# Both output products of a mixing block from three products of rounded parts, and ScalarE scaling the recurrences' outputs by their deviations

## The chip, the cores and the metric

The kernel runs on one core of a Trainium2 chip. The metric is the device time of one execution in microseconds. Times are medians of a few executions of the same program; a profile is one further execution, with its own time. Engine names are those of the profile: PE is TensorE (PEld its weight loads), DVE is VectorE, ACT is ScalarE, POOL is GpSimd, SP is SyncE, which issues most DMA transfers.

## The reference

Two transformer-like blocks on one sequence of 1024 tokens with 1024 features, all in float32. The first block mixes an attention branch and a recurrent branch. What matters here is how their outputs are made and joined:

```python
def direction(dlo, glo, w0_d, w2_d, g2_d, reverse):
    ...
    o = wkv7_scan(rh, heads(decay), kh, vh, -kk, b_vec, reverse)
    o = (head_group_norm(o, ln_g, ln_b) + bonus).reshape(B, S, RWKV_WIDTH)
    g = jax.nn.sigmoid(glo) @ g2_d
    return o.astype(cols.dtype) * g
...
o_b = fwd + bwd
y_a = o_a @ w_o_l[:MLA_WIDTH]          # attention's output, 512 -> 1024
y_b = o_b @ w_o_l[MLA_WIDTH:]          # recurrence's output, 512 -> 1024
gates = jax.nn.sigmoid(gate_cols.reshape(B, S, N_BRANCHES, D) + b_gate[l])
x = x + (gates[:, :, 0] * y_a + gates[:, :, 1] * y_b) @ w_merge[l]
```

`head_group_norm` subtracts each head's mean (8 heads of 64), divides by its deviation, multiplies by a gain and adds a bias. After this come a feed-forward layer, and a second block with gated linear attention, a convolution and another feed-forward layer; the change doesn't touch them.

## The kernel before

The program is written engine by engine: for each engine one function lists its instructions in order, with waits on semaphores (`wait_ge`, L136). Nothing reorders them: an engine that waits holds everything behind it. Tokens go in 8 tiles of 128.

*Recurrences and attention* (about 530 to 1292 us). Two recurrences (forwards `scan(e, 0)`, backwards `scan(e, 1)`) and the attention run at once, as three Python generators per engine which `scans` (L1889) steps in turn: after seven steps that the first recurrence and the attention take ahead, a round is one step of the first recurrence, one of the second, one of the attention. A recurrence has 28 steps for a tile of tokens. So the place of every instruction in an engine's stream is fixed by counting steps. The attention needs fewer steps and ends before the recurrences; its generator then takes one more step, the first part of `outa`. On SyncE that part waits for the attention's end on three engines and for its last stores to `oa_d`, and then loads the attention's output, transposed (`OAT3`, 2 MB), the gate inputs, norm gains, four tiles of `w_o` and four of the gates. On the other engines it does nothing.

*Output stage* (1292 to 1422 us). When both recurrences are over, `var_ve` and `var_ae` make the reciprocal deviations `VR` (one column per direction, tile and head). Then `by_turns` (L1914) alternates two generators on TensorE, VectorE and SyncE:

- `gn_*` handles one token tile, in the order `TORD` = 3, 4, 2, 5, 1, 6, 0, 7. TensorE makes the two directions' gate products and, later, transposes the result. VectorE, for each direction, multiplies by the deviations, by the gain `LG`, adds `bon` (GpSimd's bonus plus bias), multiplies by the gate product in PSUM, and then adds both directions into `acc`. ScalarE copies the transposes out of PSUM, feature-major, into `OBT`.
- `outa_*` is the attention's output product: 16 units (8 feature tiles, 2 halves of the tokens) of four 128x512 float32 products. VectorE multiplies each by its gate from PSUM (an "evacuation") into `mix`.

Four `outa` units go with the first tile, two with each further one. TensorE's transposes of a tile wait for `acc`; they stand in its stream behind the `outa` units of that turn and ahead of the next tile's gate products.

- `outb_*` follows: the recurrence's output product, again 16 units of four float32 products. The last token tile's transposes stand behind its second unit. For each unit VectorE multiplies by the gate (`ty`), adds to `mix`, waits for ScalarE's rounded copy of the sum and subtracts that from the sum (`lo`), so that the merge has its operand in two rounded parts.

SyncE loads `w_o`'s second half during the sixth norm tile, and x again during `outb`. Then comes the merge product (`tok_pe`), whose products are rounded ones (type fp32r) throughout: a value is split into a high part, rounded by a ScalarE copy, and a low part, the difference; the product is the sum of three products, high x high, high x low and low x high. ScalarE and VectorE split the merge's weights, one tile of 128x1024 ahead (`Split`); the tile for TensorE's second step of the merge is split behind VectorE's last `outb` unit.

A float32 product in the source (`mm`, L366) shows as two records in TensorE's timeline, a rounded one as one.

Of the kernel before, what the change touches and what calls it, by code (L numbers as in the profile page):

```python
# [235 lines left out]
def program(nc, a, out):  # L236
    ctx = ExitStack()
    with ctx:
# [11 lines left out]
        room.close()  # L250
        X = region(ctx, "X", 8192)
# [29 lines left out]
        HI.insert(0, region(room, "HI0", 1024, FR))  # L281
        room.close()
# [1527 lines left out]
        GT = [HT[:, 4096 + 512 * i:4608 + 512 * i] for i in range(4)]  # L1810
        WO = [HT[:, 6144 + 512 * i:6656 + 512 * i] for i in range(4)]
        OAT3 = v3(HT[:, 0:4096], 4)
# [4 lines left out]
        OBT = [EX[:, 2048:3072], EX[:, 3072:4096], AR[:, 12288:13312], AR[:, 13312:14336]]  # L1817
        TORD = (3, 4, 2, 5, 1, 6, 0, 7)
        WFIRST = AR[:, 14336:15360]
# [10 lines left out]
        def outa_sp(sp):  # L1830
            def load(n):
                if n >= 4:
                    sp.wait_ge(*at("pe_mix", "a", 2 * (n - 4) + 1))
                sp.e.dma_start(WO[n % 4], a["w_o"][n][:, 0:512]).then_inc(*dma(f"dma_wo{n % 4}", n))

            def gate(i):
                if i >= 4:
                    sp.wait_ge(*at("ve_mix", "a", i - 4))
                sp.e.dma_start(GT[i % 4], g_d[i // 2, i % 2]).then_inc(*dma(f"dma_gt{i % 4}", "a", i))

            for g in ("pe", "ve", "ae"):
                sp.wait_ge(*end("att", g))
# [8 lines left out]
            sp.e.dma_start(G2[1], a["g2"][128:256, :]).then_inc(*dma("dma_ln", "all"))  # L1851
            for n in range(4):
                load(n)
            for i in range(4):
                gate(i)
            yield
            for n in range(8):
# [20 lines left out]
        def outa_ve(ve):  # L1878
            yield
# [23 lines left out]
        def nothing():  # L1903
            while True:
                yield
# [79 lines left out]
        def gn_ae(ae):  # L1985
            stored(ae, 0)
            for t in TORD:
                yield
# [6 lines left out]
            yield  # L1995
# [1807 lines left out]
```

## Time and profile before

| | us |
|---|---|
| median of 3 executions | 3272.03 |
| lowest, highest | 3270.03, 3272.25 |
| the profiled execution | 3276.29 |
| its span, first to last instruction | 3274.5 |

| engine | busy us | share of the span |
|---|---|---|
| TensorE | 3153.8 | 96% |
| VectorE | 2084.6 | 64% |
| ScalarE | 1297.0 | 40% |
| GpSimd | 887.3 | 27% |

Busy time is the sum of an engine's instruction durations; matmul ends are modelled and overlap the next start, so the distance from one start to another is the safer reading of a matmul's price. A row of a timeline gives start, duration, engine, line, operation, output and inputs, and in brackets how long the engine had been idle before it and what released it. Consecutive equal instructions are merged and their number is given (x16).

### The profile page before, as it was taken

What the parts mean: (1) busy time and instruction counts of PE and PEld (TensorE: products, weight loads), DVE (VectorE), ACT (ScalarE), POOL (GpSimd) and SP (SyncE); (2) the same over time, 40 slices, a digit from 0 to 9 for tenths busy, and PEclk for the clock granted to TensorE, in tenths of its full rate; (3) what the DMA queues carried; (4) which work ended last, traced back from release to release, by engine and by line L of the source; (5) the groups of instructions that cost most, each with busy time, mean ns of one, the idle gap of its engine ahead of it and who ended that gap; (6) DMA issues with size and microseconds to landing.
All of it is one profiled execution on the core that took longest, in us unless ns stands there. A gap on an engine that the chain in (4) does not pass through costs nothing.

```text
span 3274.5 us, 61761 instructions
## 1 busy us (share of the span) xinstructions
PE 3153.8 (96%) x26560; PEld 2540.2 (78%) x26560; DVE 2084.6 (64%) x3031; ACT 1297.0 (40%) x2289; POOL 887.3 (27%) x778
## 2 busy tenths in 40 slices
PE   8999999999999988999999999999999999999998
PEld 8678776778887776467888888878677878888887
DVE  5263465666776665847899877762455575565686
ACT  4333334555555432124333344443333343333444
POOL 1232233222322222100576740000000025566100
PEclk9999999999999999999999999999999999999999
DMA  4251245112211121532123247522102322322753
GB/s 151 68 155 49 71 161 178 42 41 64 71 54 46 66 94 44 209 131 91 71 105 117 97 154 247 165 95 89 36 32 74 132 87 85 120 101 97 264 160 116
DMA packets 128016, 346.46 MB, mean 106 GB/s; under 512 B 15792, under 2 KB 19520, under 8 KB 124928
## 3 DMA queue, kind: packets, MB, share of 16 engines
q1 hardware_dynamic: 106592, 258.09, 23.7%
q0 software_dynamic: 21152, 84.42, 6.9%
q8 instruction: 210, 3.44, 0.4%
q14 instruction: 62, 0.51, 0.1%
HBM read 246.51 MB, written 95.94 MB: 105 GB/s over the span
## 4 chain that ended last, share of the span: by engine, by line
PE 83%; DVE 9%; ACT 4%; issue 2%; DMA 1%; POOL 0%; SPq 0%; DVEq 0%; ACTq 0%; POOLq 0%
PE ps L369 42%; PE ps L368 39%; PE ps L372 3%; DVE X L378 2%; DVE AR L378 2%; DVE SM L389 1%; DVE W L378 1%; DVE WS L378 1%; ACT HT L1240 1%; ACT AR L375 1%; DVE EX L378 0%; ACT WS L375 0%; ACT W L2219 0%; DMA AR<-rw_d 0%; DVE HT L382 0%
## 5 line engine op out<-in xcount | busy, mean ns | idle before, releaser
L378 DVE TENSOR_TENSOR WS<-W,WS 128x512 fp32r<-128x512 f32 (+1 forms) x284 | 341.4, 1203 | 251.1 <-ACT WS L375 250.9
L368 PE MATMUL ps<-HH,WS 128*128 128x512 f32 x1280 | 394.1, 389 | 0.0
L368 PE MATMUL ps<-TO,WS 128*128 128x512 f32 x1440 | 345.9, 389 | 0.0
L375 ACT ACTIVATE WS<-W 128x512 fp32r<-128x512 f32 (+1 forms) x284 | 210.0, 740 | 315.2 <-PE ps L369 170.9
L368 PEld LDWEIGHTS ps<-TO,WS 128*128 128x128 f32 x1440 | 270.3, 188 | 56.1
L368 PEld LDWEIGHTS ps<-HH,WS 128*128 128x128 f32 x1280 | 240.2, 188 | 49.9
L368 PE MATMUL ps<-HL,WS 128*128 128x512 f32 x640 | 249.0, 389 | 0.0
L368 PE MATMUL ps<-TO 128*128 128x512 f32 x936 | 226.8, 390 | 0.2 <-DVE TO L378 0.2
L369 PE MATMUL ps<-AR 64*64 64x64 f32 (+2 forms) x5440 | 204.1, 242 | 21.4 <-ACT AR L375 9.6
L368 PE MATMUL ps<-WS 128*128 128x512 f32 x888 | 215.1, 390 | 0.1
L375 ACT ACTIVATE X<-ps 128x512 f32<-128x512 f32 (+1 forms) x168 | 100.5, 598 | 284.5 <-PE ps L369 128.6
L369 PE MATMUL ps<-HL,HI 128*128 128x512 f32 (+1 forms) x512 | 209.1, 408 | 2.8 <-POOL WL L378 2.8
L369 PE MATMUL ps<-WS,HH 128*128 128x512 f32 x640 | 203.0, 393 | 4.5 <-DVE X L378 1.5
L369 PE MATMUL ps<-WS,HL 128*128 128x512 f32 x576 | 206.3, 392 | 0.7 <-DVE X L378 0.7
L369 PE MATMUL ps<-HH,WS 128*128 128x512 f32 (+1 forms) x672 | 205.6, 395 | 1.2 <-ACT HH L375 1.2
L369 PE MATMUL ps<-HH,HI 128*128 128x512 f32 (+1 forms) x512 | 205.7, 402 | 0.0
L369 PE MATMUL ps<-HH,WL 128*128 128x512 f32 (+1 forms) x512 | 205.5, 401 | 0.0
L368 PEld LDWEIGHTS ps<-TO 128*128 128x128 f32 x936 | 175.2, 188 | 37.1 <-DVE TO L378 1.0
L369 PEld LDWEIGHTS ps<-AR 64*64 64x64 f32 (+1 forms) x5440 | 157.1, 137 | 56.7 <-issue 29.2
L368 PEld LDWEIGHTS ps<-WS 128*128 128x128 f32 x888 | 166.3, 188 | 34.8 <-DVE WS L378 0.5
L375 ACT ACTIVATE AR<-ps 128x512 f32<-128x512 f32 (+4 forms) x240 | 124.3, 523 | 164.0 <-PE ps L369 105.2
L378 POOL TENSOR_TENSOR X<-X 128x1024 f32<-128x1024 f32 (+1 forms) x44 | 104.9, 2386 | 296.5 <-DVE X L378 225.4
(367 smaller groups left out, 6409.2 us busy)
## 6 DMA issues: line engine op xcount, KB each, us to landing
AR_b<-h_d SPq DMA_DIRECT2D x154, 256.0 KB, 2.9
AR<-rw_d SPq DMA_DIRECT2D x104, 256.0 KB, 4.1
W<-in_w_fg SPq DMA_DIRECT2D x44, 512.0 KB, 3.8
W<-in_w_fu SPq DMA_DIRECT2D x44, 512.0 KB, 4.9
h_d<-FST POOLq DMA_DIRECT2D x20, 1024.0 KB, 4.4
x_d<-X POOLq DMA_DIRECT2D x24, 512.0 KB, 4.6
W<-in_w_tok SPq DMA_DIRECT2D x24, 512.0 KB, 4.0
rw_d<-X POOLq DMA_DIRECT2D x40, 256.0 KB, 3.3
```

The lines of the kernel that those rows point to most:

```text
L368: return pe.e.matmul(o, l, r, start=start, stop=stop, skip_group_check=True)
L369: return pe.e.matmul(o, l, r, start=start, stop=stop)
L372: return pe.e.transpose(o, i, ident)
L375: return e.e.activation(o, x, ACT.Copy)
L378: return e.e.tensor_tensor(o, x, y, op)
L389: return e.e.tensor_reduce(o, x, AX.X, op)
L1240: ae.e.activation(APB[i % 2], ps[:, b:b + 2, :].rearrange("p a b -> p (a b)"), ACT.Exp, bias=sm(264 + i % 4, 1), scale=SCALE, accum_out=sm ...
```

## The change

Both output products are made from three products of rounded parts in place of one float32 product.

- *Attention's output.* Behind the attention's generator, ScalarE (`att_out_ae`) makes the rounded high part of `OAT3` in eight copies of 128x512, one a step, and GpSimd (`att_out_ge`) the low part in eight subtractions. SyncE's loads of `w_o` and of the gates move from there behind the first recurrence's generator (`wo_first_sp`), where they wait for that recurrence's end on four engines; behind the same generator, after one more step, ScalarE and GpSimd split the first four weight tiles, one a step. The other four are split during the norm tiles (`wo_hi`, `wo_lo`). Weight and gate buffers lie elsewhere.
- *Deviations.* ScalarE multiplies the recurrences' outputs by `VR`, head by head (16 copies of 128x64 with a scale for a tile, two tiles ahead), in place of VectorE's two products per tile.
- *Recurrence's output.* ScalarE copies each transposed tile twice, rounded (`OBH`) and as it is (`OBR`), both now token-tile by token-tile (512 columns in a row), GpSimd subtracts (`OBL`), and TensorE reads the four tiles of a half with a stride (`by_feature`). `w_o`'s second half is split by ScalarE (five copies during the seventh tile, three during the eighth) and GpSimd (`wb_lo`).
- *x again.* The rounded parts lie in x's place, so x is loaded after the last `outb` unit, between the merge's weight loads.

The diff, without the new memory regions and the renamed calls:

```diff
-        GT = [HT[:, 4096 + 512 * i:4608 + 512 * i] for i in range(4)]
-        WO = [HT[:, 6144 + 512 * i:6656 + 512 * i] for i in range(4)]
-        OAT3 = v3(HT[:, 0:4096], 4)
+        GT = [AR[:, 10240 + 512 * i:10752 + 512 * i] for i in range(4)]
+        WO = [AR[:, 8192 + 512 * i:8704 + 512 * i] for i in range(4)]
+        WOL = [WS[:, 512 * i:512 * i + 512] for i in range(4)]
+        WOH = [HL[:, 4096 + 512 * i:4608 + 512 * i] for i in range(4)]
+        OAT3, OAL3, OAH3 = v3(HT[:, 0:4096], 4), v3(HH[:, 0:4096], 4), v3(HH[:, 4096:8192], 4)
-        OBT = [EX[:, 2048:3072], EX[:, 3072:4096], AR[:, 12288:13312], AR[:, 13312:14336]]
+        OBR, OBL = (EX[:, 2048:4096], AR[:, 12288:14336]), (OBL0, OBL1)
+        OBH = (XF[:, 0:2048], XF[:, 2048:4096])
+        WBH = [XF[:, 4096 + 512 * t:4608 + 512 * t] for t in TORD]
+        WBR, WBL = [[z[:, 512 * n:512 * n + 512] for n in range(8)] for z in (W, WL)]
...
+        def by_feature(z):
+            return z.rearrange("p (t k n) -> p k t n", t=4, k=4)
+
...
+        def att_out_sp(sp):
             for g in ("pe", "ve", "ae"):
                 sp.wait_ge(*end("att", g))
...
+        def att_out_ae(ae):
+            for k in range(4):
+                for h in range(2):
+                    ae.wait_ge(*at("dma_oat", 0))
+                    cp(ae, OAH3[:, k, half(h)], OAT3[:, k, half(h)]).then_inc(*ae.sig("ae_mix", "oh", k, h))
+                    yield
+
+        def att_out_ge(ge):
+            for k in range(4):
+                for h in range(2):
+                    ge.wait_ge(*at("ae_mix", "oh", k, h))
+                    tt(ge, OAL3[:, k, half(h)], OAT3[:, k, half(h)], OAH3[:, k, half(h)].bitcast(F32),
+                       ALU.subtract).then_inc(*ge.sig("ge_mix", "ol", k, h))
+                    yield
+
+        def wo_first_sp(sp):
+            for g in ("pe", "ve", "ae", "ge"):
+                sp.wait_ge(*end("scan0", g))
             for n in range(4):
-                load(n)
+                outa_load(sp, n)
             for i in range(4):
-                gate(i)
+                outa_gate(sp, i)
             yield
+
+        def wo_hi(ae, n):
+            ae.wait_ge(*at(f"dma_wo{n % 4}", n))
+            if n >= 4:
+                ae.wait_ge(*at("pe_mix", "a", 2 * (n - 4) + 1))
+            cp(ae, WOH[n % 4], WO[n % 4]).then_inc(*ae.sig("ae_mix", "wh", n))
+
+        def wo_lo(ge, n):
+            ge.wait_ge(*at("ae_mix", "wh", n))
+            tt(ge, WOL[n % 4], WO[n % 4], WOH[n % 4].bitcast(F32), ALU.subtract).then_inc(*ge.sig("ge_mix", "wl", n))
+
+        def wo_first_ae(ae):
+            for n in range(4):
+                yield
+                wo_hi(ae, n)
+
+        def wo_first_ge(ge):
+            for n in range(4):
+                yield
+                wo_lo(ge, n)
+
+        def outa_sp(sp):
             for n in range(8):
                 if n + 4 < 8:
-                    load(n + 4)
+                    outa_load(sp, n + 4)
                 for h in range(2):
                     if 2 * n + h + 4 < 16:
-                        gate(2 * n + h + 4)
+                        outa_gate(sp, 2 * n + h + 4)
                     yield
 
         def outa_pe(pe):
-            yield
             for n in range(8):
-                w3 = v3(WO[n % 4], 4)
+                wh, wl = v3(WOH[n % 4], 4), v3(WOL[n % 4], 4)
                 for h in range(2):
                     b = take(pe, "outa", n, h)
-                    pe.wait_ge(*at(f"dma_wo{n % 4}", n))
-                    pe.wait_ge(*at("dma_oat", 0))
+                    pe.wait_ge(*at("ge_mix", "wl", n))
+                    pe.wait_ge(*at("ge_mix", "ol", 3, 1))
                     for k in range(4):
-                        x = mm(pe, ps[:, b, :], w3[:, k, :], OAT3[:, k, half(h)], k == 0, k == 3)
+                        mm(pe, ps[:, b, :], wh[:, k, :], OAH3[:, k, half(h)], k == 0, False)
+                        mm(pe, ps[:, b, :], wh[:, k, :], OAL3[:, k, half(h)], False, False)
+                        x = mm(pe, ps[:, b, :], wl[:, k, :], OAH3[:, k, half(h)], False, k == 3)
                     x.then_inc(*pe.sig("pe_mix", "a", 2 * n + h))
                     yield
 
...
-        def scans(e, scan, att, outa):
-
-            def att_and_loads():
+        def scans(e, scan, att, after_att, after_first):
+
+            def first_scan():
+                yield from scan(e, 0)
+                e.close("scan0", e.name)
+                yield from after_first(e)
+
+            def att_then():
                 yield from att(e)
                 e.close("att", e.name)
-                next(outa)
-
-            s0, s1, at_ = scan(e, 0), scan(e, 1), att_and_loads()
+                yield from after_att(e)
+
+            s0, s1, at_ = first_scan(), scan(e, 1), att_then()
...
-                    v = VR[:, d * 64 + t * 8:d * 64 + t * 8 + 8]
                     ve.wait_ge(*at(f"dma_of{t}", "all"))
                     ve.wait_ge(*at("dma_ln", "all"))
-                    tt(ve, v3(ot, 8), v3(ot, 8), bl(v, 64), ALU.mult).then_inc(*ve.sig("ve_mix", "n", t, d))
-                    ve.wait_ge(*at("ve_mix", "n", t, d))
+                    ve.wait_ge(*at("ae_mix", "n", t, d))
...
         def gn_ae(ae):
+            def scaled(t):
+                for d in range(2):
+                    ae.wait_ge(*at(f"dma_of{t}", "all"))
+                    ae.wait_ge(*at("ve_mix", "var"))
+                    for h in range(8):
+                        o, v = OF[d][:, t * 512 + 64 * h:t * 512 + 64 * h + 64], d * 64 + t * 8 + h
+                        x = ae.e.activation(o, o, ACT.Copy, scale=VR[:, v:v + 1])
+                    x.then_inc(*ae.sig("ae_mix", "n", t, d))
+
             stored(ae, 0)
-            for t in TORD:
-                yield
+            made = 0
+            scaled(TORD[0])
+            scaled(TORD[1])
+            for n, t in enumerate(TORD):
                 ae.wait_ge(*at("pe_mix", "gT", t))
-                for j in range(2):
-                    x = cp(ae, (EX[:, 2048:4096], AR[:, 12288:14336])[j].rearrange("p (a b) -> p a b", a=2)[:, :, t * P:(t + 1) * P],
-                           v3(ps[:, bank("gnT", t), 256 * j:256 * j + 256], 2))
-                    if j:
-                        x.then_inc(*ae.sig("ae_mix", "gT", t, frees=("gnT", t)))
-            yield
+                cp(ae, of_tile(OBH, t), ps[:, bank("gnT", t), :]).then_inc(*ae.sig("ae_mix", "gh", t))
+                cp(ae, of_tile(OBR, t), ps[:, bank("gnT", t), :]).then_inc(*ae.sig("ae_mix", "gT", t, frees=("gnT", t)))
+                if n < 4:
+                    wo_hi(ae, n + 4)
+                if n + 2 < NT:
+                    scaled(TORD[n + 2])
+                while made < (0, 0, 0, 0, 0, 0, 5, 8)[n]:
+                    ae.wait_ge(*at("dma_wob", 7))
+                    cp(ae, WBH[made], WBR[made]).then_inc(*ae.sig("ae_mix", "bh", made))
+                    made += 1
+
+        def ob_lo(ge, t):
+            ge.wait_ge(*at("ae_mix", "gT", t))
+            tt(ge, of_tile(OBL, t), of_tile(OBR, t), of_tile(OBH, t).bitcast(F32), ALU.subtract).then_inc(*ge.sig("ge_mix", "ob", t))
+
+        def wb_lo(ge, n):
+            ge.wait_ge(*at("ae_mix", "bh", n))
+            tt(ge, WBL[n], WBR[n], WBH[n].bitcast(F32), ALU.subtract).then_inc(*ge.sig("ge_mix", "bl", n))
 
...
+                if n >= 2:
+                    ob_lo(ge, TORD[n - 2])
+                if 1 <= n < 5:
+                    wo_lo(ge, n + 3)
+            wb_lo(ge, 0)
+            ob_lo(ge, TORD[6])
+            for n in range(1, 5):
+                wb_lo(ge, n)
+            ob_lo(ge, TORD[7])
+            for n in range(5, 8):
+                wb_lo(ge, n)
 
...
-                        for t in range(3):
-                            sp.e.dma_start(xt(t), a["x"][t * P:(t + 1) * P, :]).then_inc(*dma(f"dma_x{t}", "again"))
-                    if h == 0 and n >= 3:
-                        sp.e.dma_start(xt(n), a["x"][n * P:(n + 1) * P, :]).then_inc(*dma(f"dma_x{n}", "again"))
+
+        def x_again(sp):
+            sp.wait_ge(*at("pe_mix", "b", 1, 7))
+            for t in range(NT):
+                sp.e.dma_start(xt(t), a["x"][t * P:(t + 1) * P, :]).then_inc(*dma(f"dma_x{t}", "again"))
 
         def outb_pe(pe, gn):
             for h in range(2):
                 for n in range(8):
                     if h == 0 and n == 2:
                         next(gn)
-                    w3 = v3(W[:, 512 * n:512 * n + 512], 4)
+                    wh, wl, oh, ol = v3(WBH[n], 4), v3(WBL[n], 4), by_feature(OBH[h]), by_feature(OBL[h])
                     b = take(pe, "outb", h, n)
-                    pe.wait_ge(*at("dma_wob", 7))
+                    o = v3(ps[:, b, :], 4)
+                    pe.wait_ge(*at("ge_mix", "bl", n))
                     pe.wait_ge(*at("ae_mix", "gT", 7 if h else 0))
                     for k in range(4):
-                        x = mm(pe, ps[:, b, :], w3[:, k, :], OBT[k][:, half(h)], k == 0, k == 3)
+                        mm(pe, o, wh[:, k, :], oh[:, k], k == 0, False)
+                        mm(pe, o, wl[:, k, :], oh[:, k], False, False)
+                    pe.wait_ge(*at("ge_mix", "ob", 7 if h else 0))
+                    for k in range(4):
+                        x = mm(pe, o, wh[:, k, :], ol[:, k], False, k == 3)
                     x.then_inc(*pe.sig("pe_mix", "b", h, n))
...
-            weights_sp(sp, 1, first["1"])
+            weights_sp(sp, 1, 5)
+            x_again(sp)
+            weights_sp(sp, 5, first["1"])
```

## Rows read from the trace of the kernel before

**Rows 1.** The page's part 4: the chain that ended last, share by engine.

```profile
PE 83%; DVE 9%; ACT 4%; issue 2%; DMA 1%; POOL 0%; SPq 0%; DVEq 0%; ACTq 0%; POOLq 0%
```

**Rows 2.** Timeline of TensorE: start, us, engine, line, operation, shapes, count [idle before].

```profile
1310.78 0.66 PE L372 MATMUL ps<-CS,AR 128*128 128x128 f32 x4 [2.70 <-DVE AR L378]
...
1312.99 7.03 PE L369 MATMUL ps<-HT 128*128 128x512 f32 x16
...
1319.86 0.60 PE L372 MATMUL ps<-CS,AR 128*128 128x128 f32 x4
...
1320.30 1.88 PE L369 MATMUL ps<-W,AR 128*128 128x512 f32 x4
...
1322.02 7.03 PE L369 MATMUL ps<-HT 128*128 128x512 f32 x16
...
1364.97 0.60 PE L372 MATMUL ps<-CS,AR 128*128 128x128 f32 x4
...
1422.10 0.79 PE L369 MATMUL ps<-WS,HL 128*128 128x512 f32 x1
```

**Rows 3.** Busy time by stretch: us, then PE, PEld, DVE, ACT, POOL, clock, DMA.

```profile
1700.00:1800.00 100.00, 100.00 (x442) 82.78 (x442) 92.15 (x76) 38.08 (x65) 71.89 (x46) 1.00 0.31 115
```

**Rows 4.** Timeline of VectorE in the norm tiles.

```profile
1322.03 1.64 DVE L378 TENSOR_TENSOR X<-X,W 128x512 f32<-128x512 f32 x1
...
1328.53 1.28 DVE L378 TENSOR_TENSOR AR<-HT,ps 128x512 f32<-128x512 f32 x2
...
1332.11 0.69 DVE L378 TENSOR_TENSOR X<-X,AR 128x512 f32<-128x512 f32 x1
```

**Rows 5.** Timeline of GpSimd in the norm tiles.

```profile
1321.53 1.59 POOL L378 TENSOR_TENSOR AR<-AR,W 128x512 f32<-128x512 f32 x1
...
1328.76 1.04 POOL L378 TENSOR_TENSOR AR<-AR,SM 128x512 f32<-128x512 f32 x1 [5.64 <-DVE AR L378]
...
1347.26 1.27 POOL L378 TENSOR_TENSOR AR<-AR,W 128x512 f32<-128x512 f32 x1
```

**Rows 6.** Timeline of ScalarE, and of SyncE's queue at 1137.34, in the recurrences.

```profile
1135.65 0.60 ACT L375 ACTIVATE X<-ps 128x512 f32<-128x512 f32 x1 [0.49 <-PE ps L369]
...
1137.34 0.37 SPq L1845 DMA_DIRECT2D HT<-oa_d  x1
...
1138.25 0.63 ACT L1714 ACTIVATE AR<-AR 128x512 f32<-128x512 f32 x1 [2.00 <-DVE AR L378]
...
1144.07 0.60 ACT L375 ACTIVATE AR<-ps 128x512 f32<-128x512 f32 x1 [1.16 <-PE ps L369]
...
1281.07 0.38 ACT L375 ACTIVATE AR<-ps 128x256 f32<-128x256 f32 x1 [3.69 <-PE ps L369]
```

**Rows 7.** DMA issues, 1136 to 1142: count, KB each, us from issue to landing.

```profile
HT<-oa_d SPq DMA_DIRECT2D x1, 2048.0 KB, 8.0
```

**Rows 8.** Timeline of TensorE and GpSimd behind the attention's end.

```profile
1140.48 0.59 PE L369 MATMUL ps<-AR 64*64 64x64 f32 x13 [1.51 <-ACT AR L375]
...
1143.14 2.54 POOL L378 TENSOR_TENSOR AR<-AR 128x512 f32<-128x512 f32 x2 [7.91 <-PE ps L368]
...
1146.05 1.09 PE L372 MATMUL ps<-CS,AR 128*128 128x128 f32 x8
...
1154.82 0.33 PE L368 MATMUL ps<-AR,X 128*64 128x64 f32 x3 [1.67 <-issue]
```

**Rows 9.** Groups of instructions, shapes apart: count | busy us, mean ns | idle before.

```profile
L375 ACT ACTIVATE HL<-AR 128x512 fp32r<-128x512 f32 x12 | 7.6, 630 | 27.4 <-DVE AR L378 27.4
...
L375 ACT ACTIVATE W<-ps 64x128 f32<-64x128 f32 x32 | 8.7, 272 | 13.0 <-PE ps L369 12.6
...
L378 POOL TENSOR_TENSOR SPLIT<-AR,SPLIT 128x512 fp32r<-128x512 f32 x14 | 18.8, 1343 | 36.5 <-ACT SPLIT L375 36.5
```

**Rows 10.** Busy time by stretch, as Rows 3.

```profile
1156.00:1160.00 4.00, 4.00 (x84) 2.70 (x78) 1.94 (x5) 1.44 (x3) 0.00 (x0) 0.66 1.05 390
```

**Rows 11.** Timeline of VectorE at the end of the first recurrence.

```profile
1279.00 0.69 DVE L389 TENSOR_REDUCE SM<-AR 128x8 f32<-128x512 f32 x1 [1.15 <-POOL AR L378]
```

**Rows 12.** Line 1834 (loads of w_o, 256 KB): its eight landings.

```profile
DMA to landing us min/median/max: 3.2/7.9/11.4
```

**Rows 13.** Timeline of VectorE in the recurrence's output units.

```profile
1376.45 0.68 DVE L378 TENSOR_TENSOR W<-HT,ps 128x512 f32<-128x512 f32 x1
...
1379.16 0.68 DVE L378 TENSOR_TENSOR W<-HT,ps 128x512 f32<-128x512 f32 x1
...
1425.77 1.23 DVE L378 TENSOR_TENSOR WS<-W,WS 128x1024 fp32r<-128x1024 f32 x1 [0.26 <-ACT WS L375]
```

More of the change, by code:

```diff
@@ L250, in program @@
         room.close()
+        room = ExitStack()
+        XF = region(room, "XF", 8192, FR)
+        room.close()
         X = region(ctx, "X", 8192)
@@ L281, in program @@
         HI.insert(0, region(room, "HI0", 1024, FR))
+        room.close()
+        room = ExitStack()
+        region(room, "AR_e", 4096)
+        OBL1 = region(room, "OBL1", 2048, FR)
+        region(room, "AR_f", 8192 + 2048)
+        OBL0 = region(room, "OBL0", 2048, FR)
         room.close()
@@ L1828, in half, with of_tile, outa_load, outa_gate @@
             return slice(512 * h, 512 * h + 512)
[L1830 to L1839, printed above, removed]
+        def of_tile(z, t):
+            return z[t // 4][:, 512 * (t % 4):512 * (t % 4) + 512]
+        def by_feature(z):
+            return z.rearrange("p (t k n) -> p k t n", t=4, k=4)
+        def outa_load(sp, n):
+            if n >= 4:
+                sp.wait_ge(*at("pe_mix", "a", 2 * (n - 4) + 1))
+            sp.e.dma_start(WO[n % 4], a["w_o"][n][:, 0:512]).then_inc(*dma(f"dma_wo{n % 4}", n))
+        def outa_gate(sp, i):
+            if i >= 4:
+                sp.wait_ge(*at("ve_mix", "a", i - 4))
+            sp.e.dma_start(GT[i % 4], g_d[i // 2, i % 2]).then_inc(*dma(f"dma_gt{i % 4}", "a", i))
+        def att_out_sp(sp):
             for g in ("pe", "ve", "ae"):
@@ L1852, in outa_sp @@
+        def wo_first_sp(sp):
+            for g in ("pe", "ve", "ae", "ge"):
+                sp.wait_ge(*end("scan0", g))
             for n in range(4):
-                load(n)
+                outa_load(sp, n)
             for i in range(4):
-                gate(i)
+                outa_gate(sp, i)
             yield
+        def wo_hi(ae, n):
+            ae.wait_ge(*at(f"dma_wo{n % 4}", n))
+            if n >= 4:
+                ae.wait_ge(*at("pe_mix", "a", 2 * (n - 4) + 1))
+            cp(ae, WOH[n % 4], WO[n % 4]).then_inc(*ae.sig("ae_mix", "wh", n))
@@ L1857, in outa_sp @@
+        def wo_lo(ge, n):
[7 more added lines that the diff above has]
+            for n in range(4):
+                yield
+                wo_lo(ge, n)
+        def outa_sp(sp):
             for n in range(8):
                 if n + 4 < 8:
-                    load(n + 4)
+                    outa_load(sp, n + 4)
@@ L1901, in scans, with nothing @@
             e.close("scans", e.name)
-        def nothing():
-            while True:
-                yield
+        def nothing(e):
+            return iter(())
         def scans_done(e):
@@ L1985, in gn_ae @@
         def gn_ae(ae):
+            def scaled(t):
[6 more added lines that the diff above has]
+                    x.then_inc(*ae.sig("ae_mix", "n", t, d))
             stored(ae, 0)
-            for t in TORD:
-                yield
+            made = 0
+            scaled(TORD[0])
+            scaled(TORD[1])
+            for n, t in enumerate(TORD):
                 ae.wait_ge(*at("pe_mix", "gT", t))
-                for j in range(2):
-                    x = cp(ae, (EX[:, 2048:4096], AR[:, 12288:14336])[j].rearrange("p (a b) -> p a b", a=2)[:, :, t * P:(t + 1) * P],
-                           v3(ps[:, bank("gnT", t), 256 * j:256 * j + 256], 2))
-                    if j:
-                        x.then_inc(*ae.sig("ae_mix", "gT", t, frees=("gnT", t)))
-            yield
+                cp(ae, of_tile(OBH, t), ps[:, bank("gnT", t), :]).then_inc(*ae.sig("ae_mix", "gh", t))
[14 more added lines that the diff above has]
+            tt(ge, WBL[n], WBR[n], WBH[n].bitcast(F32), ALU.subtract).then_inc(*ge.sig("ge_mix", "bl", n))
         def gn_ge(ge):
@@ L3581, in tensor_program @@
             prep_pe(pe)
-            scans(pe, scan_pe, att_pe, outa)
+            scans(pe, scan_pe, att_pe, nothing, nothing)
             gn = gn_pe(pe)
@@ L3610, in vector_program @@
             prep_over(ve)
-            scans(ve, scan_ve, att_ve, outa)
+            scans(ve, scan_ve, att_ve, nothing, nothing)
             scans_done(ve)
@@ L3638, in scalar_program @@
             prep_over(ae)
-            scans(ae, scan_ae, att_ae, nothing())
+            scans(ae, scan_ae, att_ae, att_out_ae, wo_first_ae)
             scans_done(ae)
             var_ae(ae)
-            for _ in gn_ae(ae):
-                pass
+            gn_ae(ae)
             outb_ae(ae, sp)
@@ L3667, in gpsimd_program @@
             prep_over(ge)
-            scans(ge, scan_ge, att_ge, nothing())
+            scans(ge, scan_ge, att_ge, att_out_ge, wo_first_ge)
             scans_done(ge)
@@ L3687, in sync_program @@
             prep_sp(sp)
-            scans(sp, scan_sp, att_sp, outa)
+            scans(sp, scan_sp, att_sp, att_out_sp, wo_first_sp)
             gn = gn_sp(sp)
```

## The prediction

> **What bounds the kernel now.** I read the page's chain first: TensorE holds 83% of what ended last [rows 1]. The changed code lies between 1133 and 1430 us, so each price below is read there, stage by stage.
>
> *The output stage* (1292 to 1422). In TensorE's timeline [rows 2] the attention's output products are f32, two records each: 16 records, eight products, start at 1312.99 and the next instruction at 1319.86, so 0.859 us a product. A tile of the group norm takes 9.02 us (the first transposes at 1310.78, the seventh set at 1364.97: 54.19 for six), all of it TensorE: 0.44 transposes, 1.72 gate products (1319.86, 1320.30, 1322.02), 6.86 output products. The recurrence's products follow, 16 units of 3.43 us, to 1422.10, 57.1 after the seventh transposes. What a rounded product costs is read where nothing else runs: 442 in 100 us [rows 3], at most 0.227 us each.
>
> VectorE is nearly as full there. A norm tile has nine operations of 0.69 (1332.11 [rows 4]), a pitch of 0.72, and two evacuations: 8.0 us. It stretches to about 9 because GpSimd gets in the way, and the rows give the pattern: GpSimd's operation of 1321.53 [rows 5] lasts 1.59 instead of 1.27 (1347.26) and ends at 1323.12; VectorE's, started at 1322.03, lasts 1.64 and ends at 1323.67, that is, it runs its 0.55 after GpSimd's end. They take turns, about 1.1 us for GpSimd and 0.55 for VectorE. VectorE's operations with an input from PSUM are spared: two at 1328.53 take 1.28 beside GpSimd's of 1328.76. The Trainium skill, "SBUF — State Buffer", section "Who interferes with whom", says the same: a VectorE instruction with two inputs in SBUF and a GpSimd instruction that reads SBUF shut each other out for a whole instruction. It speaks against this change, which adds GpSimd operations of just this kind; the trace agrees with it, and the sums below use the rows' 1.1 and 0.55.
>
> *The recurrences* (to 1292). There the chain hops between TensorE, ScalarE and VectorE, and a delay of an in-order engine goes straight into the end.
>
> **The change part by part.**
>
> 1. *Products.* 64 + 64 f32 products become 384 rounded ones: 128 x (0.859 - 3 x 0.227) = -22.8 us of TensorE. A norm tile falls to 0.44 + 1.72 + 24 x 0.227 = 7.6, an output unit from 3.43 to 2.73. That is an upper bound; parts 4 and 5 say what is left of it.
>
> 2. *The attention's rounding, in the recurrences' stream.* ScalarE now makes eight rounded copies directly after the attention's last step, one per round of the interleaved generators. After the attention's last copy its order [rows 6] is one step of each recurrence (ending with 1135.65), then the exponentials at 1138.25. The first new copy stands between these two, and it waits for the whole reload of the attention's output. That load was issued at 1137.34, after the stores that it reads, and landed 8.0 us later [rows 7]: 1145.35. With the copy's 0.63 the exponentials start at 1146.0, 7.75 late. TensorE can't fill this: it already waits 1.51 us for the copy behind the exponentials (1140.48 [rows 8]). So +7.75.
>
>    Behind it, GpSimd's eight subtractions, 1.27 (as those of 1143.14) to 1.34 [rows 8, 9] each, queue ahead of its recurrence work. The fourth waits for ScalarE's fourth copy, which stands behind that of 1144.07 (then 1151.8), so it runs to about 1154.2; the two products of 1143.14, shifted to 1150.9, start only then and end at 1156.6. TensorE wants the first for the transposes of 1146.05 (then 1153.8), the second half-way: +2.3. The squares and the next sums, behind further subtractions, give +0.6 and +0.9. Bounds 0 (if all of it finds gaps) and 5.
>
>    Clock: after TensorE's 1.67 us without work before 1154.82, put down to issue [rows 8], the mean granted clock was 0.66 in 1156 to 1160 [rows 10], between the levels of 2.4 and 1.2 GHz: 0.34 x 4 = 1.4 us of work lost. A 9 us wait should bring one such stretch, +1.4. The old wait and its stretch, -1.7 - 1.4, should go, since eight loads that filled the queues at that time move to part 3. Bounds of the three together: -3.5 to +3.
>
>    Sum 7.75 + 3.8 - 1.7 = **+9.9** (4.3 to 15).
>
> 3. *First weights, at the end of the recurrences.* SyncE's four weight and four gate loads wait for the first recurrence on every engine; the last is VectorE's reduction of 1279.00, ended 1279.69 [rows 11]. This load landed in 3.2 at its fastest [rows 12]; in the quiet here I take 2.8, so 1282.6. ScalarE's first weight copy (0.63 [rows 9]) stands right ahead of the second recurrence's copy of 1281.07 [rows 6]: that goes to 1283.2, **+2.2** (1.5 to 3). The other three copies fit into ScalarE's waits that follow.
>
> 4. *Norm tiles.* VectorE loses two operations of nine. ScalarE gains 16 scalings of 128x64 a tile; no row has one, the nearest is 0.272 for 64x128 [rows 9], so at most 4.4 a tile; with two copies from PSUM and a weight copy it stays under 6.3 and runs two tiles ahead: hidden. (The Trainium skill, "ScalarE: Activation LUTs", section "What ACT_TABLE_LOAD costs", has a formula by which these would follow each other every 0.24 us, 3.8 a tile: the same verdict.) First tile: TensorE's first four units end 2.9 earlier, but the tile waits for its load and now for eight scalings, about 2 us, in which VectorE waited for GpSimd anyway: I get the first sum 0.9 earlier, **-0.9** (-2 to 0).
>
>    From there GpSimd has four operations a tile (three from the sixth on) in place of two. Worked through in turns: the second tile, with four evacuations first, costs VectorE 2.5, seven operations and three lost turns, 10.3 instead of 9.08; the next three 7.85 each; the last two 8.1. Sum 50.05 against 54.19: **-4.1**. Bounds: TensorE's own 7.6 throughout, -8.5, and -1.
>
> 5. *The recurrence's products.* The first unit waits for a copy and a subtraction of its weights after the seventh transposes, 1.8 us; the second 0.6; the last transposes come 9.9 after the seventh. TensorE would finish 48.6 after the seventh transposes instead of 57.1. But VectorE's units [rows 13] are 2.71 us long without GpSimd (1376.45 to 1379.16), as long as TensorE's 2.73, and begin late: the first needs a ScalarE copy that stands behind the last weight copies (13.2 after the seventh transposes), and the next three take turns with GpSimd's seven subtractions. VectorE starts unit five at 23.2 and, never catching up, ends at 57.2. The merge's second weight split comes behind it (now 1.23 at 1425.77, just in time) and is done at 59.0; TensorE wants it at 54.1. So the merge resumes 3.6 us earlier than now: **-3.6** (-8.5 to -1).
>
> 6. *x reloaded later.* SyncE issues eight loads of 512 KB after the last unit, ahead of the merge's fifth later weight load. At the rate of the reload of 2048 KB [rows 7] they take 16 us at most; the merge's first evacuation needs x only after 96 products, 21.8 us, its fifth later split at 27: nothing.
>
> **Sum.** 9.9 + 2.2 - 0.9 - 4.1 - 3.6 = +3.5. The profiled execution took 3276.29 (span 3274.5), 4.3 above the median of 3272.03; I add to the median: 3275.5.
>
> **Rivals.**
> A. *GpSimd hides.* If the subtractions mostly meet VectorE's PSUM operations and waits, TensorE bounds the stage: -8.5 in part 4, -8.5 in part 5, total 9.9 + 2.2 - 0.9 - 17 = -5.8, 3266. For it: two evacuations and two of seven operations are spared. Against: the turns [rows 4, 5].
> B. *Slower, from the recurrences.* GpSimd's late products make both recurrences wait again, and the old issue wait stays: part 2 at 15, part 3 at 3, the rest as forecast: +9.4, 3281; with VectorE's late start also 3 worse, 3284. It decides once part 2 exceeds 13. For it: eight subtractions of 1.3 us in as many rounds, each ahead of recurrence work. Against: GpSimd has long waits there (7.91 before 1143.14 [rows 8]).
> C. *The products aren't at the rounded price.* The recurrence's moving operand is now read as four pieces of 128 columns; at half the rate 192 products cost +44, 3316. Against: the pieces are long.
>
> **How the numbers follow.** Forecast 0.57, A 0.2, B 0.2, C 0.03. A measurement of this kernel tells 0.2%, 6.5 us, from no change. Beyond -6.5 lies half of A and a sliver: 0.12. Beyond +6.5 lie B, C and the upper tail of the forecast (0.09): 0.32. Within: 0.56. Range: from A's time to B's upper one, 3266 to 3284.
>
> **What would show it.** Right: a ScalarE wait of about 8 us on the attention's reload near 1137, with TensorE idle; TensorE's last recurrence product some 12 us later than now; norm tiles of about 8 us, ended by VectorE; VectorE operations of 1.2 us and more beside GpSimd; a TensorE wait of some 5 us on the merge's second split. Wrong: norm tiles of 7.6 with TensorE unbroken (A); a delay at the end of the recurrences far from 12 us (parts 2, 3); rounded products slower than 0.227 in the recurrence's units (C).

## The result and the profile after

The changed kernel takes 3277.31 us (median of 18 runs, 3272.40 to 3281.47), the kernel before on the same chips 3271.84 (18 runs). The ratio is 1.0018, 95% interval 1.0011 to 1.0025: 5.5 us slower. The interval lies clear of 1, but the difference is less than the 0.2% named ahead as what can be told from no change. The profiled execution took 3274.67, span 3272.7. A single span is no measure of so small a change: the attention's last copy by ScalarE comes at 1125.32 in it and at 1133.55 before, and in all ten profiles of this case it lies between these two, though the change touches no instruction ahead of it. So both traces are read from that copy on, stage by stage.

The page of the changed kernel, part 1 (busy us, share, instructions) and the first line of part 4 (as [rows 1]):

```profile
PE 3133.3 (96%) x26688; PEld 2565.4 (78%) x26688; DVE 2086.3 (64%) x3015; ACT 1343.0 (41%) x2441; POOL 935.4 (29%) x810
...
PE 82%; DVE 9%; ACT 4%; issue 2%; DMA 2%; POOL 0%; SPq 0%; DVEq 0%; ACTq 0%
```

TensorE did lose work, and the time didn't follow. The timeline of ScalarE around the attention's end and at the recurrences' end (the counterpart of [rows 6]):

```profile
1125.32 0.28 ACT L384 ACTIVATE HT<-ps 128x128 f32<-128x128 f32 x1 [2.17 <-PE ps L378]
...
1139.05 0.63 ACT L384 ACTIVATE HH<-HT 128x512 fp32r<-128x512 f32 x1 [11.03 <-DMA HT<-oa_d]
1139.58 0.61 ACT L1723 ACTIVATE AR<-AR 128x512 f32<-128x512 f32 x1
...
1288.12 0.63 ACT L384 ACTIVATE HL<-AR 128x512 fp32r<-128x512 f32 x1 [5.09 <-DMA AR<-in_w_o]
```

The first rounded copy keeps ScalarE waiting 11.03 us for the reload, and the exponentials of L1723 stand behind it: 14.26 us after the attention's last copy instead of 4.70. Line 1867, the reload (the counterpart of [rows 7]):

```profile
DMA to landing us min/median/max: 9.9/9.9/9.9
```

The timeline of GpSimd, and of TensorE and VectorE (the counterparts of [rows 8, 11]); the last two lines are the first recurrence's last reduction and the gates' first product:

```profile
1148.32 1.27 POOL L387 TENSOR_TENSOR HH<-HT,HH 128x512 fp32r<-128x512 f32 x1 [3.56 <-ACT HH L384]
1149.55 2.93 POOL L387 TENSOR_TENSOR AR<-AR 128x512 f32<-128x512 f32 x2
...
1141.80 0.97 PE L378 MATMUL ps<-AR 64*64 64x64 f32 x13 [11.06 <-ACT AR L384]
...
1150.86 0.66 PE L381 MATMUL ps<-CS,AR 128*128 128x128 f32 x4 [1.69 <-POOL AR L387]
...
1284.66 0.69 DVE L398 TENSOR_REDUCE SM<-AR 128x8 f32<-128x512 f32 x1 [1.15 <-POOL AR L387]
...
1299.91 1.98 PE L378 MATMUL ps<-W,AR 128*128 128x512 f32 x4 [0.40 <-DVE W L387]
```

The two products that TensorE needs stand behind a subtraction until 1149.55. Busy time by stretch (columns as [rows 3]; the clock is the third number from the right):

```profile
1135.00:1140.00 5.00, 0.00 (x0) 0.00 (x0) 0.00 (x0) 0.95 (x2) 0.23 (x1) 0.55 1.02 396
1140.00:1145.00 5.00, 3.20 (x64) 3.12 (x66) 2.37 (x3) 2.96 (x7) 3.53 (x3) 0.50 0.39 145
1145.00:1150.00 5.00, 4.18 (x94) 3.74 (x90) 2.82 (x6) 3.03 (x6) 1.69 (x2) 0.93 0.01 2
1150.00:1155.00 5.00, 3.03 (x46) 2.49 (x50) 2.82 (x4) 0.79 (x2) 5.00 (x5) 0.76 0.15 56
1155.00:1160.00 5.00, 4.82 (x134) 4.36 (x126) 4.22 (x10) 2.77 (x8) 5.00 (x6) 0.90 0.81 249
```

While TensorE stands still the granted clock falls to its level of 1.2 GHz (0.50), and the first 3.9 us of work behind the wait, to 1145.7, run at it. Behind the waits of 1.69 us (1150.86) and 1.11 us (1152.62) it falls to that level a second time, for 3.4 us until 1156.

The timeline of TensorE in the output stage (the counterpart of [rows 2]): first, second, third and seventh transposes, and the merge's second weight:

```profile
1317.75 1.11 PE L381 MATMUL ps<-CS,AR 128*128 128x128 f32 x4 [4.93 <-DVE AR L387]
...
1328.12 0.60 PE L381 MATMUL ps<-CS,AR 128*128 128x128 f32 x4
...
1335.77 0.60 PE L381 MATMUL ps<-CS,AR 128*128 128x128 f32 x4
...
1366.47 0.66 PE L381 MATMUL ps<-CS,AR 128*128 128x128 f32 x4
...
1425.77 0.79 PE L378 MATMUL ps<-WS,HL 128*128 128x512 f32 x1 [4.26 <-DVE WS L387]
```

From the second tile on there is no wait ahead of the transposes: 7.65 us a tile. VectorE and GpSimd beside it (the counterparts of [rows 4, 5]), then VectorE's first output unit and the merge's splits (the counterpart of [rows 13]):

```profile
1330.98 1.31 DVE L387 TENSOR_TENSOR X<-X,W 128x512 f32<-128x512 f32 x1
1332.32 1.42 DVE L387 TENSOR_TENSOR X<-X,AR 128x512 f32<-128x512 f32 x1
...
1330.44 1.29 POOL L387 TENSOR_TENSOR WS<-AR,HL 128x512 fp32r<-128x512 f32 x1 [3.74 <-ACT HL L384]
1331.70 1.49 POOL L387 TENSOR_TENSOR AR<-AR,SM 128x512 f32<-128x512 f32 x1
...
1330.25 3.93 ACT L2058 ACTIVATE X<-X,SM 128x64 f32<-128x64 f32 x16
...
1380.28 1.06 DVE L387 TENSOR_TENSOR ML<-AR,HL 128x512 fp32r<-128x512 f32 x1 [4.51 <-ACT HL L384]
...
1424.49 2.36 DVE L387 TENSOR_TENSOR WS<-W,WS 128x1024 fp32r<-128x1024 f32 x2 [0.25 <-ACT WS L384]
```

The stretches by these marks, in us. The kernel before is read at the rows shown ahead of the prediction and at these rows of ScalarE and TensorE. Its merge's second weight is the second product of the last row, 0.23 us behind the first: 1427.97.

```profile
1133.55 0.28 ACT L375 ACTIVATE HT<-ps 128x128 f32<-128x128 f32 x1 [2.18 <-PE ps L369]
...
1292.36 1.98 PE L369 MATMUL ps<-W,AR 128*128 128x512 f32 x4 [0.40 <-DVE W L378]
...
1427.74 0.61 PE L369 MATMUL ps<-WS,HL 128*128 128x512 f32 x2
```

| stretch | before | after | difference | predicted |
|---|---|---|---|---|
| attention's last copy to the first recurrence's last reduction | 145.45 | 159.34 | +13.9 | +9.9 |
| to the gates' first product | 13.36 | 15.25 | +1.9 | +2.2 |
| to the first transposes | 18.42 | 17.84 | -0.6 | -0.9 |
| to the seventh | 54.19 | 48.72 | -5.5 | -4.1 |
| to the merge's second weight | 63.00 | 59.30 | -3.7 | -3.6 |
| sum | 294.42 | 300.45 | +6.0 | +3.5 |

From there to the end they need 1846.5 us before (3274.5 - 1427.97) and 1846.9 after (3272.7 - 1425.77). The sum, +6.0, fits the medians' +5.5.

### The profile page after: what moved, and what is told of

The parts are those of the page before. It is cut to its first block, busy times and chain, and to the rows that moved or that the text cites. A ratio compares the mean times of both kernels' runs of the same rounds, so it can differ in the third digit from the quotient of the medians.

```text
span 3272.7 us, 62195 instructions
## 1 busy us (share of the span) xinstructions
PE 3133.3 (96%) x26688; PEld 2565.4 (78%) x26688; DVE 2086.3 (64%) x3015; ACT 1343.0 (41%) x2441; POOL 935.4 (29%) x810
## 4 chain that ended last, share of the span: by engine, by line
PE 82%; DVE 9%; ACT 4%; issue 2%; DMA 2%; POOL 0%; SPq 0%; DVEq 0%; ACTq 0%
PE ps L378 41%; PE ps L377 39%; PE ps L381 3%; DVE X L387 2%; DVE AR L387 2%; DVE SM L398 1%; DVE W L387 1%; DVE WS L387 1%; ACT AR L384 1%; ACT HT L1249 1%; DVE EX L387 1%; ACT WS L384 0%; DMA AR<-rw_d 0%; ACT W L2325 0%; DMA qk_d<-AR 0%
## 5 line engine op out<-in xcount | busy, mean ns | idle before, releaser
L378 PE MATMUL ps<-HH,WS 128*128 128x512 f32 (+1 forms) x736 | 230.6, 394 | 1.3 <-ACT HH L384 1.3
L384 ACT ACTIVATE AR<-ps 128x512 f32<-128x512 f32 (+4 forms) x236 | 123.4, 528 | 158.9 <-PE ps L378 99.2
```

The lines of the kernel that those rows point to most:

```text
L378: return pe.e.matmul(o, l, r, start=start, stop=stop)
L384: return e.e.activation(o, x, ACT.Copy)
```

## The experiments

"Reduction" below is the first recurrence's last one, "last copy" the attention's. Beside each time stands the median of the kernel before that was measured along with it.

**The wait for the reload.** Attention's copies and subtractions eight rounds later:

```diff
 def att_out_ae(ae):        # and att_out_ge likewise
+    for _ in range(8):
+        yield
     for k in range(4):
```

> The changed kernel with one edit: ScalarE's rounded copies of the attention's output and GpSimd's subtractions begin eight rounds later in the recurrences' stream, when the reload has landed. In the changed kernel 159.3 us pass from ScalarE's last copy of the attention (1125.32) to the first recurrence's last reduction (1284.66), against 145.5 in the kernel before (1133.55 to 1279.00). Theory (ScalarE's wait for the reload, in order, holds up both recurrences; the subtractions on GpSimd cost the rest): the wait of 11.0 us ahead of the first rounded copy is gone, those 9.6 us come back and at most 4 stay, so 147 to 152 us, and the kernel falls from 3277.3 to 3265 to 3269 us. Rival (the recurrences have slack, and the 13.9 us are the price of the copies and subtractions themselves): 157 to 160 us, and 3275 to 3279 us.

Measured: 3265.16 us against 3270.32, ratio 0.9985 (0.9976 to 0.9993), and 146.0 us from the last copy to the reduction. ScalarE, VectorE's reduction, and TensorE's clock:

```profile
1129.00 0.28 ACT L384 ACTIVATE HT<-ps 128x128 f32<-128x128 f32 x1 [2.18 <-PE ps L378]
...
1133.70 0.63 ACT L1723 ACTIVATE AR<-AR 128x512 f32<-128x512 f32 x1 [2.00 <-DVE AR L387]
...
1153.90 0.63 ACT L384 ACTIVATE HH<-HT 128x512 fp32r<-128x512 f32 x1
...
1274.96 0.69 DVE L398 TENSOR_REDUCE SM<-AR 128x8 f32<-128x512 f32 x1 [1.15 <-POOL AR L387]
...
1134.00:1139.00 5.00, 3.49 (x118) 3.25 (x114) 3.30 (x7) 2.45 (x6) 0.41 (x1) 1.00 0.92 343
```

The exponentials start 4.70 us after the last copy, as before the change, the copy waits for nothing, and the clock stays at 1.00. The time is as the theory had it. 13.4 us come back, a little more than expected (146.0 against 147 to 152): in this profile the copies and subtractions cost 0.5. In two further kernels below with the same edit the stretch is 147.7 and 149.1, so 0.5 to 3.6. That is a net price: the kernel before loses time there too (1.67 us to issue, a stretch at 0.66 [rows 8, 10]), which is gone here.

**GpSimd's turn.** Only the subtractions later:

```diff
 def att_out_ge(ge):
+    for _ in range(8):
+        yield
     for k in range(4):
```

> The changed kernel with GpSimd's eight subtractions of the attention's output begun eight rounds later, and ScalarE's copies where they are, with their wait for the reload. From ScalarE's last copy of the attention to the first recurrence's last reduction it is 159.3 us in the changed kernel, 146.0 with both late, 145.5 in the kernel before. Theory (ScalarE's wait alone moves both recurrences by all of it): 158 to 160 us. Rival (of the prediction: the wait is worth 9.6 us, and about 4 us are subtractions that stand in GpSimd's order ahead of the recurrences' products): 154.5 to 156.5 us.

Measured, in one profiled run: 155.9 us, so the rival holds. The last copy, GpSimd's products and the reduction:

```profile
1132.84 0.28 ACT L384 ACTIVATE HT<-ps 128x128 f32<-128x128 f32 x1 [2.18 <-PE ps L378]
...
1153.36 2.54 POOL L387 TENSOR_TENSOR AR<-AR 128x512 f32<-128x512 f32 x2 [18.84 <-PE ps L377]
...
1288.75 0.69 DVE L398 TENSOR_REDUCE SM<-AR 128x8 f32<-128x512 f32 x1 [1.15 <-POOL AR L387]
```

Its products start 20.52 us after the last copy (1132.84), not 24.23 (1149.55 - 1125.32). Of the 13.9 us, 3.4 (159.3 - 155.9) belong to subtractions ahead of these products; against the other three kernels that have them there (158.9 to 160.4 us) it is 3.0 to 4.5. The other 10.5 are ScalarE's wait, its clock, and the 0.5 to 3.6 that remain with everything late; no run parts them. The time of this one run, 3279.16, can't show 3 us: its last copy comes 7.5 us later than in the changed kernel's profile.

**The first weights.** Their copies and subtractions moved from the recurrences' end into the output stage:

```diff
-scans(ae, scan_ae, att_ae, att_out_ae, wo_first_ae)   # GpSimd's likewise
+scans(ae, scan_ae, att_ae, att_out_ae, nothing)
 def gn_ae(ae):
     scaled(TORD[1])
+    for n in range(4):
+        wo_hi(ae, n)
 def gn_ge(ge):             # in the loop, behind the bonus
+    if n == 1:
+        for m in range(4):
+            wo_lo(ge, m)
```

> The changed kernel with one edit: the first four copies and subtractions of w_o leave the recurrences' last rounds and stand in the output stage, the copies behind ScalarE's first 32 scalings, the subtractions behind GpSimd's second bonus. In the changed kernel the gates' first product comes 15.25 us after the first recurrence's last reduction (1284.66 to 1299.91), in the kernel before 13.36 (1279.00 to 1292.36). Theory (ScalarE's wait of 5.1 us for the first weights costs 1.9 there, and the work hides behind the first norm tile): 13.2 to 13.6 us, 17.8 us from there to the first transposes as now, and 3275 us. Rival (the price comes back in the output stage, where four more subtractions take turns with VectorE in the first two tiles): 13.2 to 13.6 us, but the second transposes come 12 to 15 us after the first instead of 10.4, and 3277 to 3281 us.

Both missed: 3285.06 us against 3270.32, ratio 1.0049 (1.0036 to 1.0061). The gates' first product does come 1.45 us earlier (13.80 us after the reduction), but the first transposes 30.09 us behind it instead of 17.84. TensorE:

```profile
1299.87 2.25 PE L378 MATMUL ps<-W,AR 128*128 128x512 f32 x4 [0.39 <-DVE W L387]
...
1317.25 1.22 PE L378 MATMUL ps<-HH,HL 128*128 128x512 f32 x2 [15.14 <-POOL WS L387]
...
1329.96 0.60 PE L381 MATMUL ps<-CS,AR 128*128 128x128 f32 x4
```

TensorE's order puts the attention's first four output units ahead of the first transposes. In the changed kernel they fill 1301.33 to 1312.82, while the first tile is being made; here they wait 15 us for the weights and the transposes wait behind them. The 1.45 us saved at the recurrences' end are paid with 12 in the output stage. Three rounds of delay save the first without the second; this kernel also has the two edits that pay (the late attention copies above, and one told below):

```diff
 def wo_first_ae(ae):       # and wo_first_ge likewise
+    for _ in range(3):
+        yield
     for n in range(4):
```

> As the kernel with both edits (late attention copies, first unit's copy first), and the first four weights' copies and subtractions begin three rounds later at the recurrences' end, so that ScalarE does not stand still for the load of the first weights (5.1 us of waiting in the changed kernel). Theory (that wait is the 1.9 us by which the gates' first product falls behind): 13.4 to 14.4 us from the first recurrence's last reduction to the gates' first product instead of 15.25, and 1 to 2 us under the kernel with both edits, 3260 to 3263 us. Rival (TensorE's first output units then wait for the weights' subtractions instead, as it did by 12 us with these behind the scalings): 18.5 to 21 us from the gates to the first transposes instead of 17.0, and no gain.

Measured: 3259.39 us against 3271.07, ratio 0.9964 (0.9952 to 0.9976). ScalarE's copies no longer wait, and the gates follow the reduction by 13.21 us, as in the kernel before (13.36). ScalarE's copy, then VectorE and GpSimd right at the gates, and as the last row VectorE's same operation without this edit:

```profile
1286.14 1.14 ACT L384 ACTIVATE HL<-AR 128x512 fp32r<-128x512 f32 x2
...
1291.97 1.37 DVE L387 TENSOR_TENSOR W<-W,SM 128x128 f32<-128x128 f32 x1
...
1291.93 1.26 POOL L387 TENSOR_TENSOR WS<-AR,HL 128x512 fp32r<-128x512 f32 x1 [1.26 <-ACT HL L384]
...
1289.95 0.29 DVE L387 TENSOR_TENSOR W<-W,SM 128x128 f32<-128x128 f32 x1
```

The first transposes come 18.35 us behind the gates, 1.1 more than without this edit, so 0.8 us are left. TensorE's units don't wait there, so the rival's reason isn't it. It is a turn: one VectorE operation at the recurrences' very end, on which the deviations wait, takes 1.37 us instead of 0.29, 1.08 more, beside GpSimd's fourth weight subtraction, which now starts just ahead of it. The two medians, 3259.39 and 3262.82, have overlapping intervals.

**Scaling on ScalarE, alone.** The kernel before with that part only:

```diff
-tt(ve, v3(ot, 8), v3(ot, 8), bl(v, 64), ALU.mult)...
+ve.wait_ge(*at("ae_mix", "n", t, d))
 def gn_ae(ae):             # scaled(t) as in the change
+    scaled(TORD[0]); scaled(TORD[1])
     ...
+        if n + 2 < NT:
+            scaled(TORD[n + 2])
```

> The kernel before with one part of the change alone: ScalarE scales the recurrences' outputs, 16 short activations a tile, and VectorE's two scalings a tile are gone; all products stay unrounded. Theory (of the prediction: before the change TensorE bounds a norm tile, so VectorE's relief is worth the first tile alone): the first transposes come 17.6 to 17.9 us after the gates' first product instead of 18.4, the tiles stay at 9.0 us, and the time is 0.5 to 1 us under that of the kernel before, about 3270 us. Rival (VectorE's turns with GpSimd bound the tiles of the kernel before too): tiles of 8.2 to 8.7 us, and 3 to 6 us under the kernel before.

Measured: 3272.23 us against 3271.07, ratio 1.0003 (0.9994 to 1.0012): nothing. The first transposes come 17.55 us after the gates (18.42 before), the tiles stay at 9.02 to 9.07. So the rival is out; the forecast 0.5 to 1 us is too small to be seen in the times. Undone in the changed kernel, the same part is worth much:

```diff
 # gn_ve of the changed kernel
-ve.wait_ge(*at("ae_mix", "n", t, d))
+tt(ve, v3(ot, 8), v3(ot, 8), bl(v, 64), ALU.mult)...
 # gn_ae: all calls of scaled() gone
```

> The changed kernel with the scaling by the deviations put back on VectorE (two operations a tile, 16 in all), and the 128 short activations of ScalarE gone. Theory (VectorE's and GpSimd's operations on SBUF exclude each other, and with four operations of GpSimd in a tile their turns already fill about 7.8 us: five of VectorE at 0.69 and four of GpSimd at about 1.1): two more of 0.69 make a tile of 9.1 to 9.3 us instead of 7.65, six tiles cost 9 more, the first tile 1 more: 3286 to 3289 us. Rival (TensorE bounds the tile, VectorE has room): tiles of 7.65 to 7.9 us, and 3277 to 3280 us.

Measured: 3293.36 us against 3270.32, ratio 1.0073 (1.0060 to 1.0085). The tiles take 11.90, 10.53, 9.80, 10.56, 9.38 and 9.40 us, the six 61.57 instead of 48.72: VectorE's turns bound them, as the theory had it, but they cost 12.9 us over six tiles where 9 were expected, since VectorE loses more in its turns than was counted. In the tile below four of its operations take 1.72, 0.81, 1.67 and 1.65 us instead of 0.69, 3.1 us more; in a tile of the changed kernel it is 1.6. VectorE, GpSimd and TensorE in that tile:

```profile
1361.55 1.67 DVE L387 TENSOR_TENSOR X<-X,W 128x512 f32<-128x512 f32 x1
1363.25 1.65 DVE L387 TENSOR_TENSOR X<-X,AR 128x512 f32<-128x512 f32 x1
...
1361.05 1.62 POOL L387 TENSOR_TENSOR AR<-AR,W 128x512 f32<-128x512 f32 x1
1362.63 1.73 POOL L387 TENSOR_TENSOR OBL<-AR,XF 128x512 fp32r<-128x512 f32 x1
...
1366.41 1.12 PE L381 MATMUL ps<-CS,AR 128*128 128x128 f32 x4 [2.70 <-DVE AR L387]
```

**ScalarE's order at the norm's end.**

```diff
-while made < (0, 0, 0, 0, 0, 0, 5, 8)[n]:
+while made < (0, 0, 0, 0, 0, 0, 7, 8)[n]:
 # ahead of the last tile's copies; and no longer in outb_ae
+if n == 7:
+    ae.wait_ge(*at("ve_mix", "sum", 0, 0))
+    cp(ae, HL3[:, 0, half(0)], mix(0, half(0)))...
```

> The changed kernel with one edit of ScalarE's order at the norm's end: the rounded copy of the first output unit stands ahead of the last tile's two copies, and seven of the second weights' eight copies (five before) behind the seventh tile. In the changed kernel VectorE waits 4.51 us for that rounded copy at 1380.28, and 48.0 us pass from the last transposes (1376.45) to the merge's splits (1424.49). Theory (VectorE's chain of units sets the stage's end): VectorE goes on at 1376.4 to 1376.6 on that scale, the wait goes, and 44 to 45 us pass from the last transposes to the splits: 3273 to 3274 us. Rival (TensorE's units, or GpSimd's subtractions for the weights, take over at once): 47 to 48 us, and 3276 to 3278 us.

Measured: 3270.97 us against 3270.32, ratio 1.0002 (0.9993 to 1.0011). From the last transposes to the splits it is 45.25 us, 2.8 less than in the changed kernel, where 3 to 4 were expected. VectorE's first unit, TensorE's wait in the merge and the clock behind it, and as the last row the clock at the same place in the changed kernel:

```profile
1381.47 1.01 DVE L387 TENSOR_TENSOR ML<-AR,HL 128x512 fp32r<-128x512 f32 x1 [0.70 <-ACT HL L384]
...
1427.97 0.50 PE L378 MATMUL ps<-WS,HL 128*128 128x512 f32 x1 [1.46 <-DVE WS L387]
...
1428.00:1431.00 3.00, 3.00 (x13) 2.46 (x14) 1.05 (x1) 0.00 (x0) 0.00 (x0) 1.00 1.01 397
...
1426.00:1429.00 3.00, 3.00 (x8) 2.33 (x9) 0.85 (x1) 0.00 (x0) 0.00 (x0) 0.50 1.03 421
```

VectorE's wait of 4.51 is down to 0.70 and TensorE's of 4.26 to 1.46: VectorE's late start did set the merge. The wait had a second price: behind its 4.26 us TensorE works at 0.50 for 3 us, behind 1.46 at 1.00, and from there to the end the profile is 1.1 us shorter (1845.8 against 1846.9). The median lies 2 us under the 3273 expected; part of that is the lower median of the kernel before (3270.32 against 3271.84).

**Both edits that pay**, the late attention copies and this order, in one kernel:

> The changed kernel with both edits that paid: attention's copies and subtractions eight rounds later, and the first output unit's rounded copy ahead of the last tile's copies. Theory (they act in different stages and add up): 146 us from the attention's last copy to the first recurrence's last reduction, and 135 to 136 us from there to the merge's splits (138.4 with the first edit alone, 137.3 with the second), so 3261 to 3264 us, 0.9970 to 0.9985 of the kernel before. Rival (TensorE's wait for the merge is set elsewhere once the stage begins earlier): 138 us there, and 3265 to 3267 us.

Measured: 3262.82 us against 3271.07, ratio 0.9969 (0.9958 to 0.9981). From the last copy to the reduction 147.7 us, from there to the splits 136.5, a little over what was expected; the time is as the theory had it. With the weights' three rounds as well it is the 0.9964 above: both are some 0.3% faster than the kernel before, where the change itself is 0.18% slower.

## Why the prediction was right, point by point

*The time.* 3275.5 was forecast, with no change as the likeliest; 3277.31 came. The mechanism was in the main the one named: TensorE loses its products, and the time is spent on ScalarE's wait in the recurrences, on GpSimd's order behind it and, at the norm's end, on VectorE's late start. Two terms were off in opposite directions, part 2 by +4.0 and the tiles of part 4 by -1.4, so that the time came within 2 us is partly luck. A sign named for being wrong came true, tiles with TensorE unbroken, and the delay at the end of the recurrences was 15.8 us (13.9 + 1.9) instead of 12.

*Part 2 was the mis-sized term*: +9.9 forecast, +13.9 measured, inside its bounds of 4.3 to 15. Its pieces as the runs separate them: the wait, 7.75 forecast, moved the exponentials by 9.56 (14.26 - 4.70); GpSimd's order, 3.8 forecast, was worth 3.4 (3.0 to 4.5). The wait failed on one row: I took the reload's 8.0 us from the one profile that I had. In the ten profiles of this case the same load lands in 8.0 to 10.3 us, in 9.5 to 10.3 in the five whose ScalarE waits for it. And of the credit of 1.7 for clock and the old issue wait nothing is left: that wait is gone from TensorE's timeline, but where one stretch with 1.4 us lost was forecast, TensorE worked at 0.50 for 3.9 us and again for 3.4, by the same sum about 3.6 lost (an estimate; no run parts it from the wait). Where ScalarE doesn't wait (the first experiment) the clock stays at 1.00 there. Rival B's point, part 2 above 13, was passed; the time stayed short of B's because part 2 did not reach B's 15, part 3 cost less than B's 3, and part 4 gave more.

*Part 3*: +2.2 forecast, +1.9 measured; the kernel with three rounds of delay takes it back. That the other three copies hide fits the 1.9.

*Part 4*: -0.9 and -4.1 forecast, -0.6 and -5.5 measured. The second tile was 10.37 (10.3 forecast). The next ones were to be 7.85 and 8.1, ended by VectorE; they are 7.64 to 7.76, TensorE unbroken. That step failed, and here rival A was right, though not in its -8.5, since the second tile is as forecast: the turns are there (1.31, 1.42 and, with the tile's sum, 0.94 in place of 0.69) but cost VectorE 1.6 us a tile, which leaves it level with TensorE's 7.65. How near that edge is, the kernel with the scalings back on VectorE shows: tiles of 9.4 to 11.9. The Trainium skill, "SBUF — State Buffer", section "Who interferes with whom", has a two-input VectorE instruction and a reading GpSimd instruction shut each other out; the trace agrees as to these pairs, and operations with an input from PSUM kept their 0.69. ScalarE's scalings were hidden: 16 in 3.93 us.

*Part 5*: -3.6 forecast, -3.7 measured. VectorE's fifth unit starts 23.6 us after the seventh transposes (1390.10; 23.2 forecast), its last subtraction ends 57.8 after them (1424.24; 57.2 forecast), and TensorE waits 4.26 us for the merge's split. ScalarE's order was named as the cause of the late start; changing it gave 2.8 us.

*Part 6*: nothing forecast, and no wait on x is seen in the stretch: from the merge's second weight on it is 1846.5 us before and 1846.9 after, and the 3 us at half clock just behind that point outweigh the 0.4.

*Rival C* is out: the recurrence's products follow each other every 0.23 us (TensorE's timeline):

```profile
1377.12 0.39 PE L378 MATMUL ps<-XF,WL 128*128 128x512 f32 x1
1377.35 0.39 PE L378 MATMUL ps<-XF 128*128 128x512 f32 x1
```

## What to carry to other kernels

Work put on an in-order engine inside a latency-bound stage costs above all what it makes others wait for: eight copies of 0.63 us, with their subtractions, cost 13.9 when the first stood ahead of its data, and 0.5 to 3.6 eight rounds later. A landing time read once is a sample; where a wait hangs on it, take the spread. And before moving work off such a stage, look at who consumes it in the next: the same weights, moved out of it, cost 12 us there to save 1.45 here.

## What was not expected of the hardware

One and the same load of 2048 KB took 8.0 to 10.3 us to land over ten profiles; 8.0 and 10.0 in the two whose kernels have the unchanged loads around it. Two profiles with equal instructions up to the attention's last copy reach it up to 8.2 us apart (1125.32 and 1133.55); why was not tried.
